# First shifted chunk of the second feed-forward computed pair by pair, with weights split and tables loaded in another order

## The reference, cut to what matters

```python
h = layer_norm(ALPHA * h + 0.5 * swiglu_ffn(h, ffn1_w13[l], ffn1_w2[l]), ln_g[l, 0], ln_b[l, 0])
h = layer_norm(ALPHA * h + token_mix(h, ...), ln_g[l, 1], ln_b[l, 1])      # the boundary that is changed
h = layer_norm(ALPHA * h + 0.5 * swiglu_ffn(h, ffn2_w13[l], ffn2_w2[l]), ln_g[l, 2], ln_b[l, 2])
```

## Time and profile before

| | us |
|---|---|
| median of 3 runs | 1696.39 (1696.27 to 1696.78) |
| profiled execution: first to last instruction (span) | 1693.3 |
| PE busy | 1635.4 (97%) |
| DVE busy | 1141.7 (67%) |
| ACT busy | 812.7 (48%) |
| POOL busy | 250.0 (15%) |

### The profile page before, as it was taken

How to read it: one execution, slowest core, us unless ns; L and a number is a source line. 1 busy time by engine, 2 the same in 40 slices (tenths; PEclk the granted TensorE clock), 3 DMA queues, 4 the chain that set the end, 5 groups by cost and what they waited for, 6 DMA issues and landing times.

```text
span 1693.3 us, 31358 instructions
## 1 busy us (share of the span) xinstructions
PE 1635.4 (97%) x12990; PEld 1577.8 (93%) x12990; DVE 1141.7 (67%) x1551; ACT 812.7 (48%) x1063; POOL 250.0 (15%) x228
## 2 busy tenths in 40 slices
PE   6999999999999999999999999998999999989998
PEld 6999998999999999998989998897999998889987
DVE  5555587786556856577777555787766568776664
ACT  5333474663344533365663335555434346654333
POOL 1000510400033000421140034242100020020000
PEclk9999999999999999999999999999999999999999
DMA  6455444444554455445355554334455533145553
GB/s 217 170 180 183 175 150 165 140 150 177 181 190 147 174 180 184 171 159 169 135 191 176 189 202 170 125 128 146 150 178 203 189 146 129 64 155 180 181 191 124
DMA packets 39153, 279.99 MB, mean 165 GB/s; under 512 B 4880, under 2 KB 6032, under 8 KB 8848
## 3 DMA queue, kind: packets, MB, share of 16 engines
q1 hardware_dynamic: 36896, 270.34, 44.9%
q0 software_dynamic: 2160, 8.29, 1.5%
HBM read 275.10 MB, written 1.05 MB: 163 GB/s over the span
## 4 chain that ended last, share of the span: by engine, by line
PE 78%; DVE 9%; ACT 7%; issue 3%; DMA 2%; POOL 2%; SPq 0%; DVEq 0%; ACTq 0%; POOLq 0%
PE bank L727 24%; PE bank L729 24%; PE bank L728 24%; DVE w_lo L2280 4%; ACT w_hi L1594 4%; DMA raw<-in_up_w 1%; ACT h L1652 1%; PE bank L1111 1%; ACT h_hi L1651 1%; POOL h L653 1%; POOL acc L658 1%; PE bank L1140 0%; PE bank L1097 0%; PE bank L1123 0%; DMA u<-upad 0%
## 5 line engine op out<-in xcount | busy, mean ns | idle before, releaser
L2280 DVE TENSOR_TENSOR w_lo<-raw,w_hi 128x2048 fp32r<-128x2048 f32 (+3 forms) x236 | 569.8, 2414 | 258.9 <-ACT w_hi L1594 258.7
L727 PE MATMUL bank<-h_hi,w_hi 128*128 128x272 f32 (+1 forms) x2280 | 655.9, 288 | 17.2 <-DVE h_lo L2426 13.5
L729 PE MATMUL bank<-h_hi,w_lo 128*128 128x272 f32 (+1 forms) x2280 | 652.8, 286 | 0.0
L728 PE MATMUL bank<-h_lo,w_hi 128*128 128x272 f32 (+1 forms) x2280 | 651.4, 286 | 0.0
L1594 ACT ACTIVATE w_hi<-raw 128x2048 fp32r<-128x2048 f32 (+4 forms) x243 | 475.6, 1958 | 361.8 <-PE bank L729 227.3
L727 PEld LDWEIGHTS bank<-h_hi,w_hi 128*128 128x128 f32 x2280 | 432.8, 190 | 23.5 <-issue 16.5
L729 PEld LDWEIGHTS bank<-h_hi,w_lo 128*128 128x128 f32 x2280 | 432.8, 190 | 0.0
L728 PEld LDWEIGHTS bank<-h_lo,w_hi 128*128 128x128 f32 x2280 | 431.7, 189 | 0.1
L727 PE MATMUL bank<-g_hi,w_hi 128*128 128x272 f32 (+1 forms) x1136 | 326.7, 288 | 7.7 <-DVE w_lo L2280 5.3
L728 PE MATMUL bank<-g_lo,w_hi 128*128 128x272 f32 (+1 forms) x1136 | 322.2, 284 | 0.0
L729 PE MATMUL bank<-g_hi,w_lo 128*128 128x272 f32 (+1 forms) x1136 | 322.2, 284 | 0.0
(11 more groups left out here) (394 smaller groups left out, 1915.5 us busy)
## 6 DMA issues: line engine op xcount, KB each, us to landing
raw<-in_up_w SPq DMA_DIRECT2D x111, 1024.0 KB, 4.8
raw<-in_down_w SPq DMA_DIRECT2D x40, 1408.0 KB, 5.9
raw<-in_in_w SPq DMA_DIRECT2D x20, 1024.0 KB, 4.8
raw<-in_up_w SPq DMA_DIRECT2D x16, 1152.0 KB, 5.1
raw<-in_out_w SPq DMA_DIRECT2D x16, 1024.0 KB, 4.7
raw<-in_even_w SPq DMA_DIRECT2D x12, 1024.0 KB, 4.8
raw<-in_last_down SPq DMA_DIRECT2D x11, 1024.0 KB, 4.8
raw<-in_odd_w SPq DMA_DIRECT2D x6, 1024.0 KB, 4.8
```

Source lines behind the costliest of these rows:

```text
L727: pe.matmul(out, w[0], x[0], start=first, stop=False)
L728: pe.matmul(out, w[0], x[1], start=False, stop=False)
L729: return pe.matmul(out, w[1], x[0], start=False, stop=last)
L2280: last = dve.tensor_tensor(lo[:, b:n], raw[:, slot, b:n], hi[:, b:n].bitcast(F32), ALU.subtract)
```

## The change

It touches only the second boundary of each of the first block's layers, and the table transfers.

1. PE: chunk 0 is computed by `shifted_pair`. Six steps of its first tile, six of its second, then the last two steps of both. Its release is signalled, and only then come the two `residual_sums`.
2. ACT: split 2 moves from behind the root to ahead of the square of the mean, and a one-column root ahead of it draws in the root's function table.
3. DVE: split 1 stands ahead of `mu`, split 2 ahead of `less_mean` 0, `by_deviation` 1 and split 3 ahead of the rest of the normalisation; then low tiles, means and deviations alternate, and `take(0)` follows the last low tile.
4. POOL: the ten tables are no longer issued together, but one each after `g_ready` reaches a count: after chunk 7 of the second feed-forward of layer 1, after chunk 8, and so on.

```diff
+                    g_at = (2 * LAYERS - 1) * FT + DEFER + 5
                     for dst, name in ((rel_a, "rel_a"), (logc, "logc"), ...
+                        pool.wait_ge(g_ready, g_at)
                         pool.dma_start(dst[:], a[name]).then_inc(tables_loaded, 16)
+                        g_at += 1
...
+            def shifted_pair(banks, slot):
+                def tile(k, e):
+                    return mm3(banks[e][:, first.lo:U], wpair(slot, 2 * k + e), upair(k), k == 0, k == KD - 1)
+                for e in range(2):
+                    for k in range(KD - 2):
+                        if e == 0:
+                            pe.wait_ge(u_ready, seen.next(u_ready))
+                        tile(k, e)
+                for k in range(KD - 2, KD):
+                    pe.wait_ge(u_ready, seen.next(u_ready))
+                    for e in range(2):
+                        last = tile(k, e)
                 return last
...
+                    if paired and c == 0:
+                        shifted_pair(ps[0:2], slot).then_inc(chunk_used, 1)
+                        residual_sums()
+                        return
...
-                ffn(T, DEFER)
+                ffn(T, DEFER, paired=True)
...
             def renormalise(l, i):                      # ScalarE
-                split_next(UP_BLOCKS, 0, 2)
+                if i != 1:
+                    split_next(UP_BLOCKS, 0, 2)
...
                 split_next(UP_BLOCKS, 0, 1)             # ScalarE, after project_out
+                act.activation(std[:, 0:1], eps[:, 0:1], ACT.Sqrt)
+                split_next(UP_BLOCKS, 0, 2)
                 residual_deviation()
...
+                if early:                               # VectorE, renormalise(take, early)
+                    split_next(UP_BLOCKS, 0, 1)
                 dve.wait_ge(mean_ready, seen.next(mean_ready))
                 dve.tensor_scalar(mu[:, lo:], ps[6][:, lo:T], 1.0 / D, None, ALU.mult).then_inc(mu_ready, 1)
-                split_next(UP_BLOCKS, 0, 1)
+                if not early:
+                    split_next(UP_BLOCKS, 0, 1)
...
                 dve.wait_ge(mu_ready, seen.next(mu_ready))
+                if early:
+                    split_next(UP_BLOCKS, 0, 2)
                 less_mean(0)
                 less_mean(1)
                 dve.wait_ge(std_ready, seen.next(std_ready))
                 dve.reciprocal(rstd[:, lo:], std[:, lo:]).then_inc(rstd_ready, 1)
                 dve.wait_ge(rstd_ready, seen.next(rstd_ready))
                 by_deviation(0)
+                if early:
+                    by_deviation(1)
+                    split_next(UP_BLOCKS, 0, 3)
+                    low_pair(0)
+                    for j in (2, 3):
+                        less_mean(j)
+                        by_deviation(j)
+                        low_pair(j - 1)
+                    low_pair(3)
+                    take(0)
+                else:
+                    ...                                 # as before
                 split_next(UP_BLOCKS, 0, 4)
                 take(1)
```

More of the change, by code:

```diff
@@ L798, in shifted_tile @@
                     last = mm3(bank[:, first.lo:U], wpair(slot, k * tiles + e), upair(k), k == 0, k == KD - 1)
+                return last
+            def shifted_pair(banks, slot):
[10 more added lines that the diff above has]
+                        last = tile(k, e)
                 return last
@@ L926, in ffn_down, with ffn @@
                     output_sum(n)
-            def ffn(n=T, shifted=0, prelude=False):
+            def ffn(n=T, shifted=0, prelude=False, paired=False):
                 def up(i, j, c=None):
@@ L2323, in shifted_tile, with low_pair, renormalise @@
                                          us(u_hi, k, lo, T - lo).bitcast(F32), ALU.mult, ALU.subtract).then_inc(u_ready, 1)
-            def renormalise(take):
+            def low_pair(j):
+                low_tile(2 * j)
+                low_tile(2 * j + 1)
+            def renormalise(take, early=False):
                 lo = first.lo
@@ L2350, in renormalise @@
                 by_deviation(0)
[L2351 to L2362, removed]
+                if early:
[9 more added lines that the diff above has]
+                else:
+                    split_next(UP_BLOCKS, 0, 2)
+                    by_deviation(1)
+                    less_mean(2)
+                    less_mean(3)
+                    by_deviation(2)
+                    by_deviation(3)
+                    split_next(UP_BLOCKS, 0, 3)
+                    low_pair(0)
+                    low_pair(1)
+                    take(0)
+                    low_pair(2)
+                    low_pair(3)
                 split_next(UP_BLOCKS, 0, 4)
@@ L2531, in copy_tile, with ffn @@
                 dve.tensor_copy(y[:, m, 0:S].rearrange("p a n -> p (a n)"), bank[:, 0:S]).then_inc(y_ready, 1)
-            def ffn(after, n=T, l=None, i=None, deferred=False):
+            def ffn(after, n=T, l=None, i=None, deferred=False, early=False):
                 def tail_product():
@@ L2545, in tail_product, with up @@
                                       g_hi[64:128, FT - 1, lo:n].bitcast(F32), ALU.subtract).then_inc(g_ready, 1)
-                def up(i, j, c):
+                def up(pair, j, c):
                     if deferred and c is not None and c < DEFER:
                         if c == 0:
-                            renormalise(take)
+                            renormalise(take, early)
                             gated(0)
@@ L2561, in up @@
                     elif c not in ((DEFER, DEFER + 1, 6) if deferred else (0,)):
-                        split_next(UP_BLOCKS if c is None else up1_blocks(c + 1), i, j + 1)
-                    nth = i * 2 + (j + 1)
+                        split_next(UP_BLOCKS if c is None else up1_blocks(c + 1), pair, j + 1)
+                    nth = pair * 2 + (j + 1)
                     if c == UP1 - 1:
@@ L2571, in up @@
                     dve.wait_ge(up_free, seen.at(up_free, nth))
-                    f = bass.ds(i * 2 + j, 1)
+                    f = bass.ds(pair * 2 + j, 1)
                     hi = g_hi[:, f, lo:n].rearrange("p a n -> p (a n)")
@@ L2916, in _ @@
                 project_out(T, l)
-                ffn(UP_BLOCKS, T, l, 2, True)
+                ffn(UP_BLOCKS, T, l, 2, True, True)
             first.lo = 0
```

## The result

The changed kernel is slower: 1704.71 us median (1704.21 to 1706.84, 4 runs) against 1696.59 for the kernel before; ratio 1.0048, 95% interval 1.0034 to 1.0062. The forecast was 1701.9, with a range from 1698.8 to 1704.2: the direction and the place were right, the size was not.

A forecast was written before the change was run, and what follows sets the result against it. PE, 97% busy, was taken as the bound. Chunk 4 later by 2.2 and 1.5 us, plus low clock 1.1 and 0.7, gave +5.5 us: 1696.4 + 5.5 = 1701.9, range 1698.8 to 1704.2.

The forecast's parts named there:

- PE's part and the sums behind: Layer 0, to chunk 2: pause and low clock gone, 3.9 us gained; POOL's later squares cost nothing more.
- DVE and ACT, step by step: Both boundaries: DVE stalls before split 3 (3.4 us, layer 0); chunk 4 is 2.2 and 1.5 us later.
- Tables: Ten table transfers issued one by one, by chunk: cost 0, bounds 0 and 2 us.
- Function table: Root's table load, 1.28 us, now in ACT's path: 0 in layer 0, already in the sum in layer 1.
- Port: Layer 0: DVE and POOL lock shared ports, so POOL's last squares meeting split 1 take 2.88 instead of 0.75 us.
- The clock again: Clock falls after the new pauses before chunk 4: 1.1 us in layer 0, 0.7 in layer 1; bounds 0 and 1.5 each.
- more lost: Rival: table transfers make weights late, or low clock falls elsewhere at later pauses; each adds 1.5 us; 1704, chance 0.09.

The follow-up runs named there:

- best_without_pair: early_split1_5 with chunk 0 tile by tile and the sums in its middle, as before the change; 1697.00 us, ratio 1.0008 to the kernel before.
- after_again: The changed kernel, unchanged, measured and profiled a second time (the second look); 1704.56 us, ratio 1.0052 to the kernel before.
- after_filled: The changed kernel plus 24 extra matmuls, results unread, ahead of PE's wait for chunk 4; 1703.27 us, ratio 1.0034 to the kernel before.
- after_tables_at_once: The changed kernel with the ten tables issued together again; 1706.56 us, ratio 1.0061 to the kernel before.
- tables_only: The kernel before with only the ten tables issued one by one; 1697.32 us, ratio 1.000.
- after_split3_first: The changed kernel with ACT's split 3 ahead of normed tiles 0 and 1; 1698.54 us, ratio 1.0011 to the kernel before.
- pair_tables: The kernel before with PE's side-by-side chunk 0 and tables one by one, old ACT and DVE orders; 1694.31 us, ratio 0.9983.
- early_split1_5: pair_tables plus DVE's split 1 ahead of the mean, the early one-column root, and ACT's split 5 ahead of the second deferred activation; 1690.57 us, ratio 0.9967.

## Why the prediction was right in place and wrong in size

- **PE's part and the sums behind.** Right. The pause and the low clock at the old place are gone, there is a wait of 1.33 us for POOL's squares, which took 2.80 us (2.9 forecast), and DVE's variance came at 344.99 (344.75 forecast).
- **DVE and ACT, step by step.** Right. The stall before split 3 was 3.36 us (3.4 forecast), split 4 of layer 0 was done at 368.60 (368.14; the boundary began 0.16 later), PE's pause there 3.03 us (3.1). Chunk 4 moved by 2.5 us (2.2 forecast) and 1.9 (1.5). Not forecast was PE's pause of 2.48 us before chunk 3 in layer 1; it moved nothing by itself, as PE then stood 2.46 us for split 4. Experiments back the reason, not the place alone: moving ACT's split 3 gave back 2.55 and 3.42 us.
- **Tables.** Right that they cost nothing. Right too that they are a gain without the new order (1.1 us at chunk 4).
- **Function table.** Right, nothing in layer 0: it ran from 341.23 to 342.51 with the one-column root at 342.52 behind it. The 1.38 us drain of the Trainium skill ("ScalarE: Activation LUTs", "What ACT_TABLE_LOAD costs") appears in no row here either; its load time of about 1283 ns does.
- **Port.** POOL's last sum of squares began at 341.37, 0.13 us behind DVE's split 1 (341.24 to 343.55), and ended at 344.17. The Trainium skill, "SBUF — State Buffer" ("SBUF: two separate sides"), says that the one of the two that begins first holds the shared ports for its whole instruction and the other stands; the trace agrees (2.80 us against 0.75 in the earlier trace rows). In best_without_pair PE and its weight load stood 2.1 and 2.5 us for this sum.
- **The clock again.** This is the step that failed: the term of 1.1 and 0.7 us, with bounds of 0 and 1.5 each. I took a low stretch to last 3.4 us. After the pause of layer 0 it lasted 6.8 us, 5.7 of them under work, and cost 2.06 us (4.56 less the 2.50 at chunk 4), above the bound. Four traces of that place agree: from chunk 4 to chunk 10 it takes 36.88 and 36.89 us with no low clock (after_again, after_filled), 37.80 with 3.4 us (after_tables_at_once) and 38.94 with 6.8 (after). So 0.9 us for a stretch of 3.4 was near the forecast; its length was not. In layer 1 the term measured 0.85 against 0.7.
- **The same step, from the other side.** I took it that the clock falls behind a long pause, in both kernels. The same pause did and did not bring it, before (tables_only) and after (after_again). So the trace that I set out from held a low clock that an execution need not have: in layer 0, whose code tables_only leaves alone, it is 1.2 us behind tables_only at chunk 10 (66.86 against 65.66). Between stretches without low clock, the changed order costs 69.24 - 65.66 = 3.6 us in layer 0 and not 2.5.
- **The range.** It had nothing for low clock in code that did not change, though this moves one execution against another by up to 4.8 us (last section). The rival "more lost", at 0.09, named low clock elsewhere, but as a consequence of the change; the changed kernel itself took 775.9 us for that part once and 773.9 once.

Put together: the sum forecast 2.2 + 1.5 + 1.1 + 0.7 = 5.5 us, and the first profile has 2.50 + 1.92 + 2.06 + 0.85 = 7.3. That alone would have given 1703.7, inside the range. The medians differ by 8.1 (and by 8.9 in the second look). Where the last microsecond lies, the runs do not settle: executions of one program spread over up to 9 us.

## What to carry to other kernels

An earlier start is worth nothing by itself: follow the chain to the first instruction that needs the slowest engine's last result, and compare there. In an in-order queue, ask of each moved instruction what it now stands behind; here a weight split that was free to run at 351 stood behind two tiles whose input came at 351.5, and another engine stood for it. Where a profile shows a low clock, work the comparison out at the full clock on both sides and put the low clock into the range, not into the sum.

## What was not expected of the hardware

- The length of a pause of PE does not settle the granted clock behind it: 3.03 us of idleness was followed by 1.00 (after_again, after_split3_first) and by 0.50 for 6.8 us (after); 2.78 us by 0.50 (before) and 2.67 by 1.00 (tables_only); 2.28 us by 0.50 in one layer of pair_tables and by 1.00 in the other. What does settle it, no run here was made to show.
- Low stretches had lengths of 3.4 or 6.8 us in all these traces, but for the one in which the program ends. From chunk 10 of layer 1 to the end, unchanged but for the table transfers, the time goes with their sum, whatever the kernel: 771.5 us with 18.9 us of low clock (early_split1_5), 773.6 to 773.9 with 21.3 or 21.4 (four traces), 774.9 and 775.4 with 25.6 (two), 775.4 to 776.3 with 28.4 or 28.5 (five). The 32 executions of the kernel before on one chip spread over 9 us (1692.24 to 1701.45); these 4.8 us are part of what can do that, the rest is not traced.
